# Retention stage of a two-block forward pass: the keys' decay product moves from VectorE to ScalarE, the rotation runs two tiles ahead in a work space of its own, and the distance decays come after the second tile's keys

## The reference, cut to what matters

```python
q, k = apply_rope(q, cos, sin), apply_rope(k, cos, sin)      # latent tokens only
dmat = jnp.where(lower, jnp.exp(diff * log_g), 0.0)          # per head, 128 x 128
scores = jnp.einsum('bhncd,bhnsd->bhncs', qc, kc) * dmat
y_intra = jnp.einsum('bhncs,bhnse->bhnce', scores, vc)
k_decay = jnp.exp((RET_CHUNK - 1 - pos)[None] * log_g[:, None])
kv = jnp.einsum('bhnsd,bhnse->nbhde', kc * k_decay[...], vc)
s_fin, s_prev = lax.scan(lambda s, kv_n: (g_chunk * s + kv_n, s), s0, kv)
y_cross = jnp.einsum('bhncd,nbhde->bhnce', qc * q_decay[...], s_prev)
```

## Time and profile before

| quantity | value |
|---|---|
| median of 3 executions | 4632.41 us |
| lowest and highest | 4631.38 and 4633.54 us |
| profiled execution, its own time | 4627.6 us |
| profiled execution, span from first to last instruction | 4625.8 us |
| mean granted TensorE clock | 0.932 of full speed |
| TensorE, VectorE, ScalarE, GpSimd busy | 89%, 57%, 32%, 14% of the span |
| retention's first pass | 2423 to 2509 us of the span |
| retention's second pass | 2509 to 2564 us of the span |

### The profile page before, as it was taken

The page is one execution under the profiler, slowest core; times in us unless marked ns, Lnnn a source line. Parts: engine busy times, 40 slices in busy tenths (PEclk is TensorE's granted clock), DMA queues, the critical chain, the costliest instruction groups (busy, mean ns, idle before and its releaser), DMA issues. The chain is left out here.

```text
span 4625.8 us, 74370 instructions
## 1 busy us (share of the span) xinstructions
PE 4097.5 (89%) x28926; PEld 3353.2 (72%) x28926; DVE 2622.9 (57%) x5009; ACT 1485.2 (32%) x3138; POOL 649.3 (14%) x862
## 2 busy tenths in 40 slices
PE   6999998868999989799987576899868999889978
PEld 5998887557888877699986233787757899865646
DVE  4568774667333348611227586777755335465746
ACT  4233321644222235411004243344434311143422
POOL 1111111000000000011123012000110124333320
PEclk9999999889999999899997687999878999999989
DMA  5544442542111144422322485444434344453234
GB/s 195 173 151 143 144 142 73 203 152 95 46 45 47 35 141 159 146 91 88 121 104 101 161 306 201 120 114 132 123 86 151 136 132 169 156 162 103 92 105 141
DMA packets 430000, 599.76 MB, mean 130 GB/s; under 512 B 168559, under 2 KB 317507, under 8 KB 427045
## 3 DMA queue, kind: packets, MB, share of 16 engines
q1 hardware_dynamic: 377101, 417.99, 29.5%
q0 software_dynamic: 50480, 174.80, 10.1%
q10 hardware_dynamic: 2088, 2.49, 0.2%
HBM read 430.45 MB, written 164.71 MB: 129 GB/s over the span
## 5 line engine op out<-in xcount | busy, mean ns | idle before, releaser
L129 PE MATMUL g_in_g_acc<-g_in_g_whi,g_in_hi 128*128 128x444 f32 (+4 forms) x960 | 356.1, 371 | 16.8 <-DVE g_in_g_wlo L117 10.2
L130 PE MATMUL g_in_g_acc<-g_in_g_wlo,g_in_hi 128*128 128x444 f32 (+4 forms) x960 | 345.2, 360 | 0.0
L131 PE MATMUL g_in_g_acc<-g_in_g_whi,g_in_lo 128*128 128x444 f32 (+4 forms) x960 | 344.6, 359 | 0.0
L129 PE MATMUL g_even_g_acc<-g_even_g_whi,h_hi 128*128 128x428 f32 (+2 forms) x800 | 292.0, 365 | 11.7 <-DVE g_even_g_wlo L117 11.7
L131 PE MATMUL g_even_g_acc<-g_even_g_whi,h_lo 128*128 128x428 f32 (+2 forms) x800 | 289.7, 362 | 0.0
L130 PE MATMUL g_even_g_acc<-g_even_g_wlo,h_hi 128*128 128x428 f32 (+2 forms) x800 | 289.3, 362 | 0.0
L129 PE MATMUL g_odd_g_acc<-g_odd_g_whi,h_hi 128*128 128x344 f32 (+3 forms) x816 | 263.9, 323 | 25.3 <-DVE g_odd_g_o L149 15.2
L1626 DVE SCALAR_TENSOR_TENSOR rows<-up_acc,up_taps,rows 128x1023 f32<-128x1023 f32 x88 | 112.8, 1282 | 286.6 <-ACT rows L1601 279.3
L130 PE MATMUL g_odd_g_acc<-g_odd_g_wlo,h_hi 128*128 128x344 f32 (+3 forms) x816 | 261.7, 321 | 0.0
L131 PE MATMUL g_odd_g_acc<-g_odd_g_whi,h_lo 128*128 128x344 f32 (+3 forms) x816 | 261.7, 321 | 0.0
L1550 PE MATMUL up_acc<-h_hi,up_w_hi 128*128 128x512 f32 x704 | 226.0, 398 | 13.9 <-DVE up_w_lo L1640 11.8
(11 more groups left out here) (640 smaller groups left out, 9769.2 us busy)
## 6 DMA issues: line engine op xcount, KB each, us to landing
rest<-in_w_down SPq DMA_DIRECT2D x66, 512.0 KB
g_in_m_w<-in_ada_w SPq DMA_DIRECT2D x24, 1024.0 KB, 5.7
up_w_buf<-in_w_up SPq DMA_DIRECT2D x42, 512.0 KB
g_odd_x<-U3p SPq DMA_DIRECT2D x24, 768.0 KB, 6.8
g_in_m_w<-in_w_ada SPq DMA_DIRECT2D x16, 1024.0 KB, 5.9
prep_near<-U2q SPq DMA_DIRECT2D x18, 896.0 KB
PD<-prep_od POOLq DMA_DIRECT2D x10, 1536.0 KB, 8.8
rwkv_xd<-PD SPq DMA_DIRECT2D x20, 768.0 KB
```

The lines of the kernel that those rows point to most:

```text
L129: pe.matmul(bank[:, :wd], hi[:, k, tt], w_hi[:, st % 2, k, :wd], start=k == 0, stop=False)
L130: pe.matmul(bank[:, :wd], hi[:, k, tt], w_lo[:, st % 2, k, :wd], start=False, stop=False)
L131: op = pe.matmul(bank[:, :wd], lo[:, k, tt], w_hi[:, st % 2, k, :wd], start=False, stop=k == KC - 1)
```

## The change

The list FIRST gets another order: rotate works two tiles ahead of the loop's step rather than one, and stands after keep; kd stands before copy; the distance decays become an entry "dist" of the list, done once in step 0, after keep of tile 1 and rotate of tile 2. The product kd moves from VectorE's `part` to ScalarE's: sixteen activations of 128x64 (two directions by eight heads), each a copy with a per-partition scale, where there were two multiplications of 128x512. It waits for the rotation by the semaphore that the transposes use, and once for the decays by a new semaphore. `tmp` gets a buffer of its own, `turn_work`. The whole diff:

```diff
--- before.py
+++ after.py
@@ -2063,18 +2063,19 @@
 
 
 
-    FIRST = (("rotate", 1), ("turn", 1), ("copy", 1), ("kd", 1), ("kv", 1), ("score", 1), ("keep", 1), ("silu", 1), ("am", 0), ("forward", 0), ("load", 5))
+    FIRST = (("turn", 1), ("kd", 1), ("copy", 1), ("kv", 1), ("keep", 1), ("rotate", 2), ("dist", 0), ("am", 0), ("score", 1), ("silu", 1), ("forward", 0), ("load", 5))
     SECOND = (("backward", 2), ("place", 2), ("qd", 2), ("out", 1), ("square", 0), ("var", 0), ("root", 0), ("y", 0), ("store", 0))
 
     def in_order(part):
 
         for t in range(-1, NTA):
             for what, later in FIRST:
-                if 0 <= t + later < NTA and (what != "rotate" or t + later >= NTC):
+                if what == "dist":
+                    if t == 0:
+                        part("dist_exp", 0)
+                        part("dist_mask", 0)
+                elif 0 <= t + later < NTA and (what != "rotate" or t + later >= NTC):
                     part(what, t + later)
-            if t == -1:
-                part("dist_exp", 0)
-                part("dist_mask", 0)
             if t == 4:
                 part("q_exp", 0)
         for n in range(-2, NTA):
@@ -2082,7 +2083,7 @@
                 if 0 <= n + later < NTA:
                     part(what, n + later)
 
-    with stage(nc, "ret", "const", "pos_in", "rope", "z_in", "exps", "dec", "kdec", "gch", "dmat", "q_exp", "qk0", "qk1", "qk2", "qk3", "v0", "v1", "v2", "v3", "v4",
+    with stage(nc, "ret", "const", "pos_in", "rope", "z_in", "exps", "dec", "kdec", "kdec_out", "gch", "dmat", "q_exp", "qk0", "qk1", "qk2", "qk3", "v0", "v1", "v2", "v3", "v4",
                "rot", "turned", "qk", "k_dec", "kv", "kv_out", "scores", "am", "silu", "state", "q_dec", "y_done", "sq", "var", "std", "y",
                "stored_even", "stored_odd") as (block, s, sb, ps):
         qk = sb("qk", [P, 4, 1024])
@@ -2107,7 +2108,8 @@
         dm = sb("dm", [P, HN, P])
         work = sb("work", [P, 2048])
         dtmp = work.rearrange("p (d h t) -> p d h t", d=2, h=HN)
-        tmp = work.rearrange("p (n h f) -> p n h f", n=4, h=16)
+        turn_work = sb("turn_work", [P, 2048])
+        tmp = turn_work.rearrange("p (n h f) -> p n h f", n=4, h=16)
         carry = sb("carry", [P, 4, HD])
         sq = sb("sq", [P, HN, HD])
         ss = sb("ss", [P, HN])
@@ -2234,6 +2236,19 @@
         @block.scalar
         def _(act):
             def part(what, t):
+                if what == "kd":
+                    if t == 0:
+                        act.wait_ge(s.kdec_out, 1)
+                    act.wait_ge(qk_in[t % 4], (t // 4 + 1) * DMA)
+                    if t >= NTC:
+                        act.wait_ge(s.rot, t - NTC + 1)
+                    if t >= 2:
+                        act.wait_ge(s.kv, t - 1)
+                    for d in range(2):
+                        for h in range(HN):
+                            e = slice(h * HD, (h + 1) * HD)
+                            op = act.activation(kd[:, t % 2, d, e], qk[:, t % 4, 512 + h * HD:512 + (h + 1) * HD], ACT.Copy, scale=kdec[:, d, h])
+                    op.then_inc(s.k_dec, 1)
                 if what == "copy":
                     act.wait_ge(s.turned, t + 1)
                     if t >= 2:
@@ -2305,14 +2320,6 @@
                     dve.tensor_tensor(b, tmp[:, 2], tmp[:, 3], ALU.add)
                     dve.drain()
                     dve.sem_inc(s.rot, 1)
-                if what == "kd":
-                    dve.wait_ge(qk_in[t % 4], (t // 4 + 1) * DMA)
-                    if t >= 2:
-                        dve.wait_ge(s.kv, t - 1)
-                    keys = qk[:, t % 4, 512:1024].rearrange("p (h d) -> p h d", d=HD)
-                    for d in range(2):
-                        op = dve.tensor_tensor(kd[:, t % 2, d].rearrange("p (h d) -> p h d", d=HD), keys, kdec[:, d].broadcast_to([P, HN, HD]), ALU.mult)
-                    op.then_inc(s.k_dec, 1)
                 if what == "dist_mask":
                     dve.wait_ge(s.dmat, 1)
                     for d in range(2):
@@ -2362,8 +2369,7 @@
             dve.drain()
             dve.sem_inc(s.dec, 1)
             dve.wait_ge(s.kdec, 1)
-            dve.tensor_scalar(kdec[:], kdec[:], HD ** -0.5, None, ALU.mult)
-            dve.drain()
+            dve.tensor_scalar(kdec[:], kdec[:], HD ** -0.5, None, ALU.mult).then_inc(s.kdec_out, 1)
             in_order(part)
```

## The result

The changed kernel takes 4652.72 us in the median of five executions (4650.53 to 4658.38), against 4632.41 us before in the same comparison (4628.71 to 4633.54, five executions). The ratio is 1.0046, with a 95% interval of 1.0035 to 1.0057: 20 us slower, where 23 were forecast. In a second, later comparison it took 4656.32 us against 4634.08, ratio 1.0049 (1.0036 to 1.0062).

The account below looks back on a forecast made before the run. VectorE was taken to set the pace, 7.0 us a tile, until kd, kv and keep form a serial loop on ScalarE. Front 8.7, steady part 11.7 and q_exp 2.5 give +23 us: 4655.4 us, range 4637 to 4666.

Parts of the forecast that it names:

- one serial loop: Retention first pass: on ScalarE, keep waits for kv, kv for kd, and the next kd stands behind keep; 8.97 us a turn.
- The price of kd: ScalarE, sixteen 128x64 activations with a per-partition scale: 0.245 us each, 3.9 us in all, bounds 2.3 and 4.8 us.
- The rival of cheap short activations: ScalarE's kd: the pointer scale hides at 64 columns, kd takes 2.3 us; +6 us, 4638 us; chance 0.14.
- The front: First pass, tile 0 to tile 2: keep 2 ends 8.7 us later, with score 1 held up by the exponentials.
- The steady part: First pass, tile 3 to tile 9: seven loop turns of 8.97 us, 62.8 against 51.1 us, +11.7 us.
- q_exp: ScalarE work hidden so far, now between keep 5 and kd 6: +2.5 us.
- three kv of four at half: TensorE, steady part: kv at half clock (3.62 us) three times in four, otherwise 2.02 us; 3.2 us in the mean.
- The sum: Whole kernel: 8.7 + 11.7 + 2.5 = +23 us, second pass only shifted; 4655.4 us against the median.
- The rival with the full clock throughout: TensorE's score and turn break up the loop so that no kv runs at half clock; +12 us, 4644 us; chance 0.12.
- the other signs that the text named: Profile after: among others, VectorE idle for a third of 2460 to 2525 us, loop turns near 9, last keep near 2532 us.
- the rotation's head start: VectorE's rotation two tiles ahead: rotations 3 to 9 cost nothing, since VectorE needs 5.4 us a tile, the loop more.
- the new place of the decays: Front: the exponentials, which held up kd 1 before, now hold up score 1; one stall traded for another.

Follow-up runs that it names:

- e3_kd_ahead: Changed kernel with kd's sixteen ScalarE activations one tile further ahead, between copy and keep, and rotation three tiles ahead; 4639.99 us, ratio 1.0015 to the kernel before.
- e5_kd_two_wide: Changed kernel with kd as two 128x512 ScalarE copies scaled by a constant, decays left out of the keys; 4624.29 us, ratio 0.9984 to the kernel before.
- e4_kd_no_pointer: Changed kernel with kd's sixteen activations scaled by a constant instead of a per-partition scale, decays left out; 4639.02 us, ratio 1.0013 to the kernel before.
- the fillers: Changed kernel with twelve extra 128x128 TensorE matmuls behind every transposed tile from tile 1; 4651.39 us, again 4652.58 us.

## Why the prediction was right

**The mechanism.** The forecast was that kd, kv and keep become one serial loop and that VectorE stops being the bound. The changed kernel's waits show it, e3_kd_ahead (the same work out of the chain: 13 us back) and e5_kd_two_wide (the same chain, short: a gain) separate it from an amount of work on ScalarE.

**The price of kd.** 3.9 us was taken for sixteen activations; they take 3.93. From start to start one takes 0.240 us with a pointer scale and 0.147 without. "VectorE: DVE Perf Modes" of the Trainium skill, in its section on the TRN2 errata of SBUF-source operations, gives 240 ns by estimate, and the trace agrees for the form with a pointer. "Perfetto Trace Analysis" of the Trainium skill, in Optimizing Scalar/DVE Operations, gives 146 ns by estimate, and the trace agrees for the form without one. The rival of cheap short activations would have given 4638 us; made true in e4_kd_no_pointer, it gave 4639. Its chance of 0.14 was a fair one: nothing in the trace had the form itself.

**The front.** Keep 2 was put 8.7 us later. It ended at 2467.35 + 1.55 = 2468.90 us, 44.0 us from the table load, against 34.7 before: +9.3. TensorE's steps there were a little longer than taken: kv 1 3.12 us instead of 2.8, score 1 2.08 instead of 1.75, kv 2 2.99 instead of 2.8.

**The steady part.** A turn was put at 8.97 us with kv at 3.2. From keep 2 to keep 9 it is 2534.48 - 2468.90 = 65.6 us, 2.6 of them for q_exp, so 63.0 us or 9.0 a turn, +11.9 in seven, where +11.7 stood. q_exp was put at +2.5 and delays kd 6 by 2.6 us. Small errors cancel: 0.18 us pass between keep and kd where 0.11 was taken, but 0.10 between kd and kv where 0.15 was taken.

kv was 3.17 us in the mean where 3.2 was taken, and that is in part luck. The text had three kv of four at half and one at full clock, from a single pause. Measured are one of seven at full (2.02), two at half (3.75) and four in between (2.74 to 3.55), in which the clock changes; in the second comparison the mean was 3.31. The kernel before already had kv of 3.43 to 3.62 us in four of these seven tiles (2.9 in the mean), three of them after a pause of only 0.64 us, so a pause just ahead of kv wasn't the whole rule.

**The sum.** +23 against +23.8 us at the last keep and 20.3 in the medians. The difference between those two lies in other stages, whose scatter is larger. The rival with the full clock throughout would be 6.5 to 8.5 us lower in this stage, as the fillers show, where its 4644 us was 11 below the forecast. Of the other signs that the text named, VectorE was idle for more than the third that it gave: busy for 36.5 of the 65 us from 2460 to 2525, it was idle for 44%.

**What it left out.** The text held that the rotation's head start costs nothing, and no run shows a cost of it by itself. It saw that the new place of the decays trades one stall for another, but didn't ask what the parts are worth alone. They aren't worth a fixed sum: the parts other than kd's move gain 3.7 us with kd on VectorE and lose 4.3 with kd on ScalarE, and kd's move costs 19.5 us on the list as before and 27.5 on the changed one. Either way it is the main loss.

## What to carry to other kernels

Moving work off the fullest engine can close a chain with what waits for it: ask what stands ahead of and behind it in the new queue, and whether its consumer's result is waited for in that same queue. If it is, add up the chain's turn and compare it with the turn of the engine that was full: 9.0 us against 7.0 lost here, 5.0 gained. Work that is too long for the chain can be issued one tile ahead, between two instructions that wait anyway; here that gave back 13 of the 20 us, but not the stall at the front. And one broadcast multiplication of 128x512 (0.65 us) doesn't equal eight activations with a pointer scale each (2.0 us): count instructions before elements. A wait that is removed is worth only what the queue behind it can't fill already.

## What the runs showed of the hardware that was not expected

A per-partition scale pointer makes a 128x64 copy on ScalarE 0.240 us from start to start instead of 0.147; the pointer adds 0.09 us to each, more than 64 columns do (0.055 us by the estimate in the prediction). And 2.84 us of matmuls that no one needs in each turn raised TensorE's mean granted clock from 0.81 to 0.97, so that kv took 2.1 us instead of 3.2 in the mean of tiles 3 to 9: the stage was 8.3 us shorter with more work in it (154.5 against 162.8 us).
